# Splitting the GpSimd subtraction of each weight slab into four pieces, in a float32 two-block transformer kernel

## The reference

```python
def first_block(x, ...):                       # two layers
    for l in range(DEPTH):
        z = rms_norm(x, g_mix_norm[l]) @ w_in[l]
        a = mla_mixer(...)                     # low-rank attention, 4 heads
        gm = sgu_mixer(...)                    # spatial gating
        po = pool_mixer(...)                   # windowed means
        x = x + concat(norms of a, gm, po) @ w_out[l]
        h = rms_norm(x, g_ffn_norm[l])
        x = x + (silu(h @ w_gate[l]) * (h @ w_up[l])) @ w_down[l]
    return x

def second_block(x, ...):                      # two layers: short convolution, dilated attention
    for i in range(DEPTH):
        mixed = short_conv_mixer(...) if i == 0 else dilated_attention_mixer(...)
        h = h + mixed
        h = h + square(relu(rmsnorm(h) @ mlp_w_up[i])) @ mlp_w_down[i]
        h = h + sigmoid(rmsnorm(h) @ ple_w_gate[i]) * (p[i] @ ple_w_proj[i])
    return rmsnorm(h, norm_final)
```

## Time and profile before

| | |
|---|---|
| median of 3 runs | 2771.72 us (2771.29 to 2781.44) |
| profiled execution | 2774.78 us, span of its instructions 2773.0 us |
| PE busy | 2633.6 us, 95% of the span |
| DVE busy | 1505.1 us, 54% |
| POOL busy | 1475.7 us, 53% |
| ACT busy | 471.5 us, 17% |
| DMA | 236.70 MB, mean 85 GB/s |
| mean granted clock of PE | 0.974 of 2.4 GHz |

### The profile page before, as it was taken

One profiled execution on the slowest core, in us unless ns is written; L12 is line 12 of the kernel. 1 busy time (PEld: TensorE's weight loads), 2 busy tenths in 40 slices (PEclk: granted clock), 3 DMA queues, 4 the chain that ended last, 5 costly groups with the idle time before them and its releaser, 6 DMA issues.

```text
span 2773.0 us, 30840 instructions
## 1 busy us (share of the span) xinstructions
PE 2633.6 (95%) x11906; PEld 2158.1 (78%) x11906; DVE 1505.1 (54%) x1678; ACT 471.5 (17%) x777; POOL 1475.7 (53%) x465
## 2 busy tenths in 40 slices
PE   7889999999899999999999999898999999999997
PEld 6658888877588888787878887687788878878875
DVE  5767454046675540457751715895379357815526
ACT  3342111022421110101100102200310042100012
POOL 4525665654266565555655655455336514656652
PEclk9899999998999999999999999999999999999998
DMA  4102223231022322232322222232112202222221
GB/s 148 61 16 96 101 91 105 92 112 62 2 105 91 106 91 96 87 104 84 108 77 105 91 98 94 75 106 76 61 46 91 106 32 81 94 78 104 91 97 54
DMA packets 36891, 236.70 MB, mean 85 GB/s; under 512 B 4048, under 2 KB 5584, under 8 KB 9168
## 3 DMA queue, kind: packets, MB, share of 16 engines
q1 hardware_dynamic: 33456, 230.78, 23.8%
q10 hardware_dynamic: 3360, 4.85, 0.6%
HBM read 233.51 MB, written 2.10 MB: 85 GB/s over the span
## 4 chain that ended last, share of the span: by engine, by line
PE 82%; DVE 11%; issue 3%; ACT 2%; DMA 1%; POOL 0%; DVEq 0%; ACTq 0%; SPq 0%; POOLq 0%
PE psum L440 25%; PE psum L441 25%; PE psum L442 25%; DVE work L1341 3%; PE psum L888 2%; DVE work L1265 2%; DVE x_low L1281 1%; PE psum L872 1%; PE psum L650 1%; DVE work L1338 1%; PE psum L897 1%; ACT mlp_high L999 1%; DVE x_res L1385 1%; PE psum L776 1%; PE psum L760 0%
## 5 line engine op out<-in xcount | busy, mean ns | idle before, releaser
L380 POOL TENSOR_SCALAR w_high<-w_stage 128x2048 fp32r<-128x2048 f32 x216 | 419.0, 1940 | 1242.1 <-PE psum L442 1230.3
L382 POOL TENSOR_TENSOR w_low<-w_stage,w_high 128x2048 fp32r<-128x2048 f32 x216 | 1026.1, 4751 | 18.0
L440 PE MATMUL psum<-x_high,w_high 128*128 128x512 f32 x2048 | 808.0, 395 | 38.5 <-DVE x_low L1281 36.9
L441 PE MATMUL psum<-x_low,w_high 128*128 128x512 f32 x2048 | 801.6, 391 | 0.0
L442 PE MATMUL psum<-x_high,w_low 128*128 128x512 f32 x2048 | 801.6, 391 | 0.0
L440 PEld LDWEIGHTS psum<-x_high,w_high 128*128 128x128 f32 x2048 | 387.6, 189 | 124.1 <-issue 31.8
L441 PEld LDWEIGHTS psum<-x_low,w_high 128*128 128x128 f32 x2048 | 387.6, 189 | 83.2 <-issue 2.4
L442 PEld LDWEIGHTS psum<-x_high,w_low 128*128 128x128 f32 x2048 | 387.2, 189 | 81.2
L1305 DVE TENSOR_TENSOR x_res<-psum,x_res 128x512 f32<-128x512 f32 x64 | 46.9, 733 | 372.5 <-PE psum L442 372.5
L440 PE MATMUL psum<-mlp_high,w_high 128*128 (+1 forms) x576 | 227.8, 396 | 14.2 <-DVE work L1338 11.0
L441 PE MATMUL psum<-mlp_low,w_high 128*128 (+1 forms) x576 | 226.7, 394 | 0.0
(11 more groups left out here) (240 smaller groups left out, 3162.8 us busy)
## 6 DMA issues: line engine op xcount, KB each, us to landing
w_stage<-in_wstream SPq DMA_DIRECT2D x216, 1024.0 KB, 4.9
x_res<-in_x SPq DMA_DIRECT2D x2, 1024.0 KB, 11.8
out_x<-attn_out SPq DMA_DIRECT2D x8, 256.0 KB, 2.1
inv_count_sb<-in_inv_count ACTq DMA_DIRECT2D x2, 512.0 KB, 8.7
ple_proj<-in_p ACTq DMA_DIRECT2D x2, 512.0 KB, 3.7
v_tok<-in_mask ACTq DMA_DIRECT2D x1, 576.0 KB, 3.9
w_spat<-in_spatial ACTq DMA_DIRECT2D x2, 256.0 KB, 5.2
diag_sb<-in_diag ACTq DMA_DIRECT2D x2, 256.0 KB, 9.4
```

Source lines behind the costliest of these rows:

```text
L380: pool.tensor_scalar(wh[:, s, :], stage[:, s, :], 1.0, 1.0, ALU.mult, ALU.mult).then_inc(high_written, 1)
L382: pool.tensor_tensor(wl[:, s, :], stage[:, s, :], wh[:, s, :].bitcast(F32), ALU.subtract) \
L440: pe.matmul(out, wa, ra, start=start, stop=False)
L441: pe.matmul(out, wa, rb, start=False, stop=False)
```

## The change

The low part of a slab is written by four instructions of 512 columns each; only the last of them raises `slab_split`. There is no wait between the four. The high part stays one instruction, and no other engine's program changes.

```diff
+LOW_PIECES = 4
...
                 pool.tensor_scalar(wh[:, s, :], stage[:, s, :], 1.0, 1.0, ALU.mult, ALU.mult).then_inc(high_written, 1)
                 pool.wait_ge(high_written, n)
-                pool.tensor_tensor(wl[:, s, :], stage[:, s, :], wh[:, s, :].bitcast(F32), ALU.subtract) \
-                    .then_inc(slab_split, 1)
+                for q in range(LOW_PIECES):
+                    part = slice(q * SLAB // LOW_PIECES, (q + 1) * SLAB // LOW_PIECES)
+                    last = pool.tensor_tensor(wl[:, s, part], stage[:, s, part], wh[:, s, part].bitcast(F32), ALU.subtract)
+                last.then_inc(slab_split, 1)
```

## The result

| | before | with the change |
|---|---|---|
| median | 2776.58 us (2771.29 to 2781.95, 4 runs) | 2730.11 us (2729.78 to 2731.37, 4 runs) |
| ratio | | 0.9839, 95% interval 0.9818 to 0.9861 |
| profiled execution | 2774.78 us, span 2773.0 | 2729.78 us, span 2728.0 |
| mean granted clock of PE | 0.974 | 0.981 |

The kernel is 1.6% faster, 46 us by these medians. Single executions of the kernel before lie in two groups, near 2771 and near 2781 us; against the lower group the gain is 41 us.

A forecast was written before the change was run, and what follows sets the result against it. PE was taken to lose time to DVE, held up by POOL's long L382. Terms 6.2 + 5.0 + 4.8 + 4.4 + 4.0 + 1.4 - 3.6 = 22.2 us gave 2750 us; range 2738 to 2762, or to 2782 with rivals.

The forecast's parts named there:

- the first: No opening between pieces: DVE waits for all four, 5.04 us instead of 4.50; 9 us slower, 2781; chance 0.20.
- POOL is not the bound: Rival for mlp up projections and attention query/key tiles: POOL becomes the bound, PE waits for slabs; 2788 and above; chance 0.08.
- The second rival: Interleaving costs more: pieces with changeovers take 1.5 us, small terms vanish, mix ends lose 2 us more; 2761; chance 0.12.
- the small terms: Gains at softmax, openings and score steps, from DVE having free time between blocked instructions; 9.8 us in all.
- the mlp's two terms: Start of the down projection, two mlp phases: shorter PE wait, 6.2 us, and PE's clock staying up, 5.0 us.
- the attention's: Attention's first batch, once: DVE no longer behind at the last query and key tile, PE restarts 4.8 us earlier.
- the loss at the ends of mix: Ends of both mix phases: PE waits for POOL itself, whose subtraction gets longer; loss of 1.8 us each, 3.6.
- the prediction's step: Attention: with the pieces DVE is on time at the end, the wait of 8.84 us for L1400 becomes 4.0.
- openings and score steps: Openings of second mix and conv, 2.0 us; of the two ple phases, 2.0; attention's first score steps, 1.4.
- softmax: Softmax of the two mix phases: L1577 ends 3.2 us earlier, interleaving costs about 1; net 2.2 each, 4.4 us.
- the end of the first ple: End of ple: four blocked instructions in a row against four pieces; gain 0, give or take 1 us.
- conv's last tile: Conv's last tile: four blocked instructions in a row against four pieces; gain 0, give or take 1 us.

The follow-up runs named there:

- e6: Pieces only in the tenth slab of each mlp phase, all other slabs subtracted whole as in the kernel before; 2762.3 us, ratio 0.9962.
- e7: Pieces only in the first nine slabs of each mlp phase, the tenth and all others whole as in the kernel before; 2755.6 us, ratio 0.9935.
- e11: Pieces only in the fourteenth slab of the attention phase, all others whole as in the kernel before; 2778.1 us, ratio 1.0003.
- e12: Pieces only in the first thirteen slabs of the attention phase, all others whole as in the kernel before; 2767.4 us, ratio 0.9963.
- e9: Changed kernel with the high part also in four pieces, both parts whole in the ninth slab of each mix phase; 2720.6 us.
- e8: Changed kernel with the ninth slab of each mix phase subtracted by one instruction; 2720.9 us, ratio 0.9804.
- e13: Pieces only in the sixth and seventh slab of both mix phases, all others whole as in the kernel before; 2770.3 us, ratio 0.9981.

## Why the prediction was wrong

**What held.** That DVE's waits for POOL's longest instruction are what PE waits for, and that DVE gets in between pieces. The piece of 1.26 us measured 1.256; it was read off a row of another shape, so some of that is luck. A DVE instruction in between costs a piece 0.45 us, within the 0.35 to 0.5 taken. Of the rivals, the first did not happen: there is an opening. POOL is not the bound: rounding and four contended pieces take 1.92 + 6.24 = 8.2 us of a slab's 10.8, where I had worked out 9.0. The second rival's condition came true, since a contended piece takes 1.7 us and it asked for 1.5, but what it drew from it did not: the small terms did not vanish, they came out larger than forecast. All seven terms have the right sign; place by place the small ones are 0.4 to 1.9 us off.

**How much was missing.** The places give 40.8 us where the sum had 22.2. Of the 18.6 us between them 6.4 lie in the mlp's two terms (wait and clock) and 5.9 in the attention's; the small terms were 8.9 too low, and the loss at the ends of mix 2.6.

**The step that failed: the sum for the mlp's down projection begins with the old timeline.** It starts with "L382 has DVE out of its way at 1419.55", the time of the trace of before, and shortens only what comes after it, as a place where DVE "has only one blocked instruction and then other things to do". But the same change had acted on every slab before that one. In the trace of before PE is done with the last up-projection tile, and begins the down projection, at 1416.84; DVE frees that tile's bank only at 1426.79:

```profile
1416.84 0.39 PE L440 MATMUL psum<-mlp_high,w_high 128*128 128x512 f32 x1
```

DVE came into the last subtraction with two tiles still in their banks (L1338 at 1419.57 and at 1426.11), because of the earlier ones. The changed kernel's timeline of DVE at the place of the earlier trace rows:

```profile
1397.31 0.69 DVE L1341 TENSOR_TENSOR work<-psum,rstd 128x512 f32<-128x512 f32 x1 [1.90 <-PE psum L445]
1398.03 1.94 DVE L1344 SCALAR_TENSOR_TENSOR work<-work 128x512 f32<-128x512 f32 x1
...
1402.74 0.69 DVE L1341 TENSOR_TENSOR work<-psum,rstd 128x512 f32<-128x512 f32 x1 [1.07 <-PE psum L445]
...
1408.19 0.69 DVE L1341 TENSOR_TENSOR work<-psum,rstd 128x512 f32<-128x512 f32 x1 [1.87 <-PE psum L445]
1408.91 1.88 DVE L1344 SCALAR_TENSOR_TENSOR work<-work 128x512 f32<-128x512 f32 x1
```

DVE now waits for PE ahead of every tile (the bracket names PSUM, written by L445), which it did not do in the window of before, and frees the last bank at 1408.88, 3.2 us before PE comes back to it at 1412.07 (the matmul that stood at 1426.85). The granted clock over the same place stays at 1.00 (compare):

```profile
1404.00:1410.00 6.00, 6.00 (x28) 4.98 (x27) 3.17 (x4) 0.63 (x1) 3.43 (x3) 1.00 0.49 168
1410.00:1415.00 5.00, 5.00 (x23) 4.13 (x22) 1.56 (x2) 0.63 (x1) 4.92 (x5) 1.00 0.04 11
```

e6 and e7 separate the two: the last slab's opening alone is worth 5.8 to 6.0 us (forecast 5.6), the earlier ones alone 8.7 to 8.9, and both together no more than the earlier ones alone. So the two terms, 11.2 us with the clock, measured 17.6, 6.4 more.

**A misread beginning of a wait.** For attention the forecast did say that with the pieces DVE is no longer behind; there it was the beginning of the sum that was wrong. I wrote that PE finishes the last query and key tile at 1898.15, which is where its wait of 8.84 us begins. PE's wait begins when it wants the bank that L1400 frees, and before that it had worked on value products in two other banks. The tile had been ready two value groups earlier, at 1892.55, where the value products begin (the two operands change places there):

```profile
1892.55 0.39 PE L440 MATMUL psum<-w_high,x_high 128*128 128x512 f32 x1
```

At that time DVE was about to take up the tile two before it (L1619 at 1892.68; the last two follow at 1900.31 and 1903.56). The changed kernel shows the distance that is needed:

```profile
1871.70 0.68 DVE L1622 TENSOR_TENSOR work<-psum,work 32x512 f32<-32x512 f32 x1 [1.65 <-PE psum L445]
...
1874.39 1.66 DVE L1627 TENSOR_TENSOR qk<-work 32x512 f32 x1
1875.98 0.14 DVE L1403 COPY stat<-psum 128x4 f32<-128x4 f32 x1
```

From the last tile to the copy DVE needs 4.4 us, blocked once for a piece, and PE, which comes to the bank at 1876.93, does not wait at all. So DVE had been two tiles behind, 6.5 us of its own work (2 x 3.25), and with the pieces it is on time. Counted from 1892.55 and not from 1898.15 the forecast's own steps would have left no wait. The term of 4.8 us measured 9.0, and 1.7 more where the clock no longer falls, which the sum had at nothing. e11 and e12 bear out the backlog, 2.0 us from the last slab and 8.1 from the thirteen before it. The rival in their expectations is called the prediction's step; for attention it was not, since that step took DVE to be on time.

**Sizes only.** The loss at the ends of mix was 6.2 instead of 3.6 us. The row of the changed kernel (POOL's four pieces merged, then PE):

```profile
188.44 6.38 POOL L385 TENSOR_TENSOR w_low<-w_stage,w_high 128x512 fp32r<-128x512 f32 x4
```
```profile
194.87 0.72 PE L443 MATMUL psum<-mla_high,w_high 128*128 128x512 f32 x1 [3.25 <-POOL w_low L385]
```

The subtraction takes 6.38 us instead of 4.88, 1.5 more (1.8 forecast). What I left out is that the wait of 3.25 us was followed by a stretch at half clock (0.62 from 194 to 198 us): the first matmul behind it takes 0.72 us and the next 0.63, where behind the wait of 1.74 us before they took 0.50 and 0.39. That is the other 1.6 us. Too low were the terms at openings and score steps (in all 5 us), softmax (1.4), and those put at nothing for the end of the first ple (1.9) and conv's last tile (0.7), where four blocked instructions against four pieces were taken to give no gain. Why each of these was too low was not worked out; e9, with the rounding in pieces too, raises the one of ple from 1.9 to 4.6.

**Outside the sum.** The upper group of executions was not in the forecast at all. It gives 4 to 5 us of the 46 between the medians. One of the three runs of before stood at 2781.4; I took that for scatter and did not ask for its cause.

## What to carry to other kernels

When two engines exclude each other instruction by instruction, cut the long instruction of the one that has time, and leave it whole at the places where its own end is waited for (e8). Two pieces took most of the gain here, and eight are not shown to take more than four. When you work out what a shorter block is worth, follow the blocked engine from where it was last on time, not from the last block ahead of the wait: a repeated block builds up lateness, and here removing all of them removed the whole wait and the fall of the clock behind it.

## What the runs showed of the hardware

- POOL gives way to a waiting DVE instruction between two of its own instructions, even where the next follows at once: pieces with no semaphore between them take 1.26 us alone and 1.71 with a DVE instruction in between. In the trace of the changed kernel no DVE instruction without a PSUM operand stretches from before the end of one piece to beyond the end of the next, save the reciprocals (L1275), which take 3.35 us with or without POOL. "GPSIMD Engine Reference" of the Trainium skill, section 2.1, on the cores that start the next instruction by themselves, had left open whether this works; the trace says that it does.
- The same instructions ran in one profile with the wait of 6.9 us and in another without it, about 10 us apart (9.5 us between e7 and before from 660 to 680 us). What differed ahead of it was PE's granted clock, 1.00 against 0.50, which moved POOL by 2.8 us, and 1.1 us of DVE. The kernels that have whole subtractions in mix like before had two groups, 2771 and 2781 us for before, and four slabs in pieces (e13) were enough to leave one.
- Waits of PE of 1.7 us (before, e6) and 2.4 us (e12) were not followed by a granted clock of 0.5, and one of 3.25 us was. The wait alone does not tell: in before PE is busy at full clock from 634 to 644 us without a wait, and has half clock from 644 to 654.
